# Head-norm averages through 32-wide groups, other slots for the sample states, and another order in the last pair of a two-layer decoder step

## What is computed

```python
# layer A, per head (4 heads of 256): norm of the gated output h
h = sigmoid(o_pre) * hs
mu = mean(h, axis=-1, keepdims=True)              # over the 256 values of a head
var = mean(square(h - mu), axis=-1, keepdims=True)
hn = (h - mu) * rsqrt(var + EPS) * g_hn
y = hn + skip * xc
# layer A, the samples' states: C (8 samples, 4 heads, 256, 256)
C_new = dc * C + ws * outer(v, k)                 # 32 states, each read, updated and written
num = ... + dec * einsum('vk,k->v', C, q)
# end of either layer
out = concat([y_mix, ym]) @ w_out
x = x + rmsnorm(out, g_post)
```

## Time and profile before

| | us |
|---|---|
| three runs | 1763.52, 1765.01 (median), 1767.86 |
| profiled execution | 1766.36 |
| its span in the trace | 1764.2 |
| busy in it: TensorE, VectorE, ScalarE, GpSimd | 1744.2, 869.8, 592.5, 499.0 |

### The profile page before, as it was taken

How to read it: one execution, slowest core, us unless ns; L and a number is a source line. 1 busy time by engine, 2 the same in 40 slices (tenths; PEclk the granted TensorE clock), 3 DMA queues, 4 the chain that set the end, 5 groups by cost and what they waited for, 6 DMA issues and landing times.

```text
span 1764.2 us, 22648 instructions
## 1 busy us (share of the span) xinstructions
PE 1744.2 (99%) x8390; PEld 1361.2 (77%) x8390; DVE 869.8 (49%) x1801; ACT 592.5 (34%) x1437; POOL 499.0 (28%) x539
## 2 busy tenths in 40 slices
PE   9999999999899999999999999999999999999998
PEld 5577766988788888747658888888888888888643
DVE  1444323785566556552333444355435544466775
ACT  2321235564465234311221223432333234533312
POOL 0251100335222002410003543145414553123630
PEclk9999999999999999999999999999999999999999
DMA  7312111247655235541111111223123343745323
GB/s 270 137 61 79 53 64 57 53 135 174 200 159 173 90 93 150 176 167 48 50 48 59 47 48 44 97 90 96 50 73 117 102 141 109 270 159 167 126 104 112
DMA packets 149079, 196.23 MB, mean 111 GB/s; under 512 B 19083, under 2 KB 108171, under 8 KB 148834
## 3 DMA queue, kind: packets, MB, share of 16 engines
q1 hardware_dynamic: 140708, 174.58, 31.2%
q10 hardware_dynamic: 8262, 20.20, 3.4%
HBM read 156.97 MB, written 37.85 MB: 110 GB/s over the span
## 4 chain that ended last, share of the span: by engine, by line
PE 90%; DVE 3%; issue 3%; ACT 1%; DMA 1%; POOL 1%; DVEq 0%; SPq 0%; ACTq 0%; POOLq 0%
PE PS L3511 51%; PE PS L2257 7%; PE PS L2407 5%; PE PS L2047 3%; PE PS L396 3%; PE PS L570 3%; PE PS L2498 2%; PE PS L2083 2%; PE PS L2058 2%; PE PS L291 2%; PE PS L2080 2%; PE PS L920 1%; DVE WK L727 1%; PE PS L913 1%; PE PS L1337 1%
## 5 line engine op out<-in xcount | busy, mean ns | idle before, releaser
L3511 PE MATMUL PS<-HT,RING 128*128 128x258 f32 (+2 forms) x1776 | 444.6, 381 | 0.3 <-ACT WK L3601 0.3
L3511 PEld LDWEIGHTS PS<-HT,RING 128*128 128x128 f32 x1776 | 329.5, 190 | 46.0 <-issue 1.1
L3601 ACT ACTIVATE BIG<-PS 128x256 f32<-128x256 f32 (+2 forms) x140 | 53.8, 385 | 382.3 <-PE PS L3511 382.2
L3511 PE MATMUL PS<-BIG,RING 128*128 128x258 f32 (+1 forms) x656 | 159.6, 382 | 0.0
L3511 PEld LDWEIGHTS PS<-BIG,RING 128*128 128x128 f32 x656 | 123.1, 190 | 17.9 <-issue 0.2
L3511 PE MATMUL PS<-BIG,WK 128*128 128x258 f32 (+1 forms) x448 | 114.2, 386 | 5.2 <-DVE BIG L3703 5.2
L3511 PE MATMUL PS<-HT,CST 128*128 128x256 f32 (+2 forms) x432 | 110.2, 382 | 0.1
L3511 PEld LDWEIGHTS PS<-BIG,WK 128*128 128x128 f32 x448 | 84.3, 193 | 17.9 <-DVE BIG L3703 5.6
L3511 PEld LDWEIGHTS PS<-HT,CST 128*128 128x128 f32 x432 | 79.6, 190 | 11.5 <-DVE BIG L3700 0.9
L570 PE MATMUL PS<-WK,RING 128*128 128x344 f32 x288 | 84.3, 453 | 0.1
L3697 DVE TENSOR_TENSOR BIG<-BIG,PS 128x256 f32<-128x256 f32 (+1 forms) x70 | 29.6, 422 | 104.8 <-PE PS L3511 104.8
(11 more groups left out here) (452 smaller groups left out, 3255.5 us busy)
## 6 DMA issues: line engine op xcount, KB each, us to landing
RING<-in_w_in_a SPq DMA_DIRECT2D x14, 1024.0 KB, 6.2
WK<-in_cache_mem_kv SPq DMA_DIRECT2D x56, 256.0 KB, 5.7
RING<-in_w_kv_b SPq DMA_DIRECT2D x12, 1024.0 KB, 5.3
RING<-in_w_in_b SPq DMA_DIRECT2D x12, 1024.0 KB, 5.2
WK<-in_cache_win SPq DMA_DIRECT2D x40, 256.0 KB, 5.1
RING<-in_w_mkv SPq DMA_DIRECT2D x16, 512.0 KB, 5.1
BIG<-in_x_prompt SPq DMA_DIRECT2D x16, 512.0 KB
BIG<-sample_query SPq DMA_DIRECT2D x28, 256.0 KB, 5.7
```

Of the source, the lines that this page charges most:

```text
L3511: last = nc.tensor.matmul(PS[:, bank, 0:mid - lo], weight_block(u // 2, s, k), h_block(layer_of(u), u % 2, t, k), start=(k == 0 and j not ...
L3601: nc.scalar.activation(part(u, n2 if j == 0 else n1, lo, mid), PS[:, banks(u)[0], 0:mid - lo], ACT.Copy).then_inc(sig("projections_copied" ...
```

## The change

Three edits.

First, an average is made in two steps. `group_sums` multiplies four quarters of the columns (258 each) with 32 columns of the averaging matrix, each quarter into 32 other partitions of bank 7; ScalarE copies them back to SBUF, scaled by 1/32 (`group_sums_act`); in the slot behind, `average` multiplies each 32 rows with ones and writes them to four banks (3 to 6) on all partitions. The root's Ln moves to VAR + 2, to the slot of its Exp.

Second, the states' slots come from a formula. For n = 0 to 23 they were 9, 12, 16, 19, 23, 26, 30, 33, 37, 40, 44, 47, 51, 54, 58, 61, 65, 68, 72, 75, 79, 82, 86, 89. They are 9, 12, 16, 24, 27, 30, 34, 37, 41, 44, 47, 51, 54, 58, 61, 64, 68, 71, 75, 78, 81, 85, 88, 92.

Third, product 2 of the last pair goes from behind `value(5)` to the end, and for the last block ScalarE and VectorE take the second half first.

```diff
@@ -115,6 +115,9 @@
...
+        def quarters(ap):
+            return ap.rearrange("p (b n) -> p b n", b=4)
+
         def vec(row, kt):
...
@@ -185,7 +188,9 @@
...
         for h in range(H):
+            job(f"sums_mean{h}")
             job(f"mean{h}", "dve")
+            job(f"sums_var{h}")
             job(f"var{h}")
...
@@ -1233,9 +1238,13 @@
...
+        def state_slot(i):
+
+            n = i - EARLY_STATES
+            return (9, 12, 16)[n] if n < 3 else 24 + 17 * (n - 3) // 5
+
         def states_at(x):
-            return [i for i in range(EARLY_STATES, H * NS)
-                    if 9 + 7 * ((i - EARLY_STATES) // 2) + 3 * (i % 2) == x]
+            return [i for i in range(EARLY_STATES, H * NS) if state_slot(i) == x]
...
@@ -1324,17 +1333,33 @@
...
-        AVERAGED = PS[:, 3:6, 0:SEG]
-
-        def average(pe, name, h, summed):
+        QUARTER = W // 4
+        AVERAGED = PS[:, 3:7, 0:QUARTER]
+
+        def group_sums(pe, name, h, summed):
...
                 pe.wait_ge(sig("c_copied").sem, H)
-            else:
+            for q in range(4):
+                last = nc.tensor.matmul(PS[32 * q:32 * (q + 1), 7, 0:QUARTER], avg_h[:, 0:32],
+                                        big(HELD[h][0], q * QUARTER, (q + 1) * QUARTER), start=True, stop=True)
+            last.then_inc(job_done.up(), 1)
+
+        def group_sums_act(act, name, h):
+
+            act.wait_ge(job_done.sem, done("sums_" + name))
+            nc.scalar.activation(big(HELD[h][0], 0, QUARTER), PS[:, 7, 0:QUARTER],
+                                 ACT.Copy, scale=1.0 / 32).then_inc(job_read["act"].up(), 1)
+
+        def average(pe, name, h):
+
+            pe.wait_ge(*read_of("sums_" + name))
+            if name != "mean0":
                 pe.wait_ge(*read_of(f"mean{h}" if name[0] == "v" else f"var{h - 1}"))
-            for b in range(3):
-                last = nc.tensor.matmul(AVERAGED[:, b, :], avg_h, big(HELD[h][0], b * SEG, (b + 1) * SEG),
+            for q in range(4):
+                rows = slice(32 * q, 32 * (q + 1))
+                last = nc.tensor.matmul(AVERAGED[:, q, :], ones[rows, :], big(HELD[h][0], 0, QUARTER)[rows, :],
                                         start=True, stop=True)
...
@@ -1345,10 +1370,16 @@
...
                 if x == MEAN[h]:
-                    average(pe, f"mean{h}", h, "values_summed")
+                    group_sums(pe, f"mean{h}", h, "values_summed")
+                    yield
+                if x == MEAN[h] + 1:
+                    average(pe, f"mean{h}", h)
                     yield
                 if x == VAR[h]:
-                    average(pe, f"var{h}", h, "squares_summed")
+                    group_sums(pe, f"var{h}", h, "squares_summed")
+                    yield
+                if x == VAR[h] + 1:
+                    average(pe, f"var{h}", h)
                     yield
...
@@ -1401,7 +1432,7 @@
...
                 act.wait_ge(sig("y_ready").sem, 2 * h - 1)
-            nc.scalar.activation(seg3(ROOT), AVERAGED, ACT.Ln, bias=EPSC).then_inc(job_read["act"].up(), 1)
+            nc.scalar.activation(quarters(ROOT), AVERAGED, ACT.Ln, bias=EPSC).then_inc(job_read["act"].up(), 1)
...
@@ -1437,11 +1468,14 @@
...
                 for h in range(H):
+                    if x == MEAN[h]:
+                        group_sums_act(act, f"mean{h}", h)
                     if x == GATE[h] + 12:
                         squares_act(act, h)
-                    if x == GATE[h] + 17:
+                    if x == VAR[h]:
+                        group_sums_act(act, f"var{h}", h)
+                    if x == VAR[h] + 2:
                         root_log(act, h)
-                    if x == GATE[h] + 18:
                         root_exp(act, h)
...
@@ -1495,7 +1529,7 @@
...
                 dve.wait_ge(job_done.sem, done(f"mean{h}"))
-                ins = nc.vector.tensor_tensor(seg3(big(6 * h + e)), seg3(big(6 * h + e)), AVERAGED, ALU.subtract)
+                ins = nc.vector.tensor_tensor(quarters(big(6 * h + e)), quarters(big(6 * h + e)), AVERAGED, ALU.subtract)
                 if e == 1:
...
@@ -2307,9 +2341,9 @@
...
                       (0, 4), (0, 1), (5, 2), (0, 3), (0, 5), (0, 6),
-                      (2, 1), (2, 4), (7, 2), (2, 3), (2, 5), (2, 6),
+                      (2, 1), (2, 4), (2, 3), (2, 5), (2, 6),
                       (5, 1), (5, 4), (5, 3), (5, 5), (5, 6),
-                      (7, 1), (7, 4), (7, 3), (7, 5), (7, 6)]
+                      (7, 1), (7, 4), (7, 3), (7, 5), (7, 6), (7, 2)]
...
@@ -2618,7 +2652,6 @@
...
             value(5)
-            pair_product(pe, p3, 2)
             pair_product(pe, p1, 3)
...
@@ -2631,7 +2664,7 @@
...
             pair_product(pe, p2, 6)
-            for j in (1, 4, 3, 5, 6):
+            for j in (1, 4, 3, 5, 6, 2):
                 pair_product(pe, p3, j)
...
@@ -2639,6 +2672,10 @@
...
                 .then_inc(sig("block_root").up(), 1)
+
+        def half_order(x, i):
+
+            return (1, 0) if x == "B" and i == NB - 1 else (0, 1)
...
@@ -2649,12 +2686,12 @@
...
                 act.wait_ge(sig("block_squares").sem, squares_of(x, i - 2, 1))
-            for half in range(2):
+            for k, half in enumerate(half_order(x, i)):
                 if x == "B":
...
                 nc.scalar.activation(junk[0:n, half * 512:(half + 1) * 512], src, ACT.Square,
-                                     accum_out=small(x, i, half)).then_inc(sig("block_squares").up(), 1)
+                                     accum_out=small(x, i, k)).then_inc(sig("block_squares").up(), 1)
             act.wait_ge(sig("block_bias").sem, nth(x, i))
...
@@ -2733,11 +2770,11 @@
...
                 dve.wait_ge(sig("block_sum").sem, nth(x, i - 2))
-            for half in range(2):
-                dve.wait_ge(sig("block_squares").sem, squares_of(x, i, half))
+            for k, half in enumerate(half_order(x, i)):
+                dve.wait_ge(sig("block_squares").sem, squares_of(x, i, k))
                 last = nc.vector.tensor_tensor(c.t(i)[0:n, halves[half]], half_of(i, half), c.post[0:n, halves[half]],
                                                ALU.mult)
-                if half == 0:
+                if k == 0:
                     nc.vector.tensor_scalar(small(x, i, 2), small(x, i, 0), 1.0 / D, EPS, ALU.mult, ALU.add)\
...
```

## The result

The changed kernel takes 1775.65 us (median of 6 runs, 1773.81 to 1779.31), the kernel before 1763.42 beside it (1759.82 to 1767.86). The ratio is 1.0070, with a 95% interval of [1.0053, 1.0088]: 12.3 us slower. The profiled execution took 1779.31 us, its span 1777.5.

A forecast was written before the change was run, and what follows sets the result against it. TensorE was busy 1744.2 of 1764.2 us, so only fewer columns or fewer waits change the time. Terms -8.5 + 11.8 + 6.6 + 1.1 + 0.3 = +11.3 on 1765.0 gave 1776.3 us, range 1767 to 1785.

The forecast's parts named there:

- (f): Whole kernel: the forecast with its small terms, clock falling in two or three waits, 1773 to 1780 us; chance 0.52.
- first wait with its clock: TensorE's wait on the C21 sum near 455, fourth state at slot 19: 5.2 plus 3.3 us go, -8.5.
- three new waits: TensorE waits for U2 at slots 38, 66, 94, behind gating of heads 1 to 3: 4.6, 4.8, 2.4 us, +11.8.
- slow clock behind them: Granted clock falls behind two of the waits for U2, 3.3 us each: +6.6; ends 0 and +9.9.
- averages: Eight averages in narrow groups: 0.83 + 1.05 = 1.88 us each against 1.74, +1.1; ends -0.6 and +9.8.
- last pair: Last stage, product (7, 2) at the end: a 1.9 us wait uncovered behind value step 5, net +0.3; ends -1, +1.
- Rival (a): Gating of heads 1 to 3: ScalarE's last sums done before VectorE asks, no new waits; -7.1, 1757.9 us; chance 0.07.
- Rival (b): Clock holds through the waits for U2, or falls once: +4.7 to +8.0, 1769.7 to 1773.0 us; chance 0.15.
- rival (e): The wait near 455 stays, loads late whatever the slot, or slots not as said: 1784.8 us; chance 0.06.
- (c): Narrow groups run at pure column time, 0.86 us per average: -7.0 instead of +1.1, 1768.2 us; chance 0.10.
- (d): The four row groups run one after another: +9.8 instead of +1.1, 1785.0 us; chance 0.10.

The follow-up runs named there:

- repaired slots alone: Kernel before with only the slots of states n = 0 to 7 changed, to 9, 12, 16, 23, 25, 28, 31, 34; ratio 0.9973 to it.
- fourth state early: Changed kernel with state slots 9, 12, 16, 19, 25, 28, 31, 34, then the old ones; ratio 0.9992 to the kernel before.
- slots alone: Kernel before with only the change's new state slots, old averages and old order of the last products; ratio 1.0073 to it.
- kernels with one late head: Changed kernel, slots 9, 12, 16, 23, 25, 28, 31, 34, then old ones, except n = 7 at 37 (1.0019) or n = 23 at 92 (0.9991 to before).
- head 3 alone late: Changed kernel with state slots 9, 12, 16, 23, 25, 28, 31, 34, then old ones, but n = 23 at 92; ratio 0.9991 to before.
- averages computed twice: Changed kernel, slots 9, 12, 16, 23, 25, 28, 31, 34, then old ones, every group sum and average done twice; ratio 1.0013 to before.

## Why the prediction was right, and where it was not

The forecast was 1776.3 us, +11.3, and the median came out at 1775.65, +12.3 by the ratio, in the case that was called likeliest (f). (The kernel before stood at 1763.42 in these runs and not at 1765.0, which is why the time looks closer than the difference.) Step by step:

| term | forecast | measured | by |
|---|---|---|---|
| first wait with its clock | -8.5 | -4.8 (trace: -8.5) | repaired slots alone; -3.7 by the fourth state early |
| three new waits | +11.8 | +12.1 (the same in slots alone) | waits of the trace |
| slow clock behind them | +6.6 | +5.35 | chain, 3 x 42 records |
| averages | +1.1 | -1.0 | chain; alone -0.9 |
| last pair | +0.3 | +0.4 | tail of the trace |
| sum | +11.3 | +12.1 | runs: +12.3 (+9.3 to +15.5) |

**The new waits** are the step that carried the result, and it held in mechanism, place and size. The engine, the two instructions and who queues behind them were as the order had shown. Per head 4.6, 4.8 and 2.4 were forecast, 5.07, 5.13 and 1.91 came. For head 1 VectorE needed longer from the end of the sums (485.30) to the end of U2 (489.6): 4.3 us where 0.79 + 2.50 + 0.42 = 3.7 was reckoned. The steps from L1506 on took 1.01 us for the 0.79, and the two multiplications (L1524) 2.91 for the 2.50 of the earlier trace rows. In the chain of the changed kernel the same stretch is 5.0 us for head 2 and 4.1 for head 3, where 4.6 was reckoned for both, so part of the good sum is that these misses cancel. Rival (a), the one on the other side, fell: ScalarE's 6.34 us of idling ahead of the copy was there, and of no use, since its queue is in order. Rival (b) had the clock fall once or never, and it fell twice; rival (e) had the first wait stay, and it went.

**The first wait** is the mis-sized term. The price was taken from one execution, 5.17 + 3.3. The place and the cause were right, and in that trace the number was too; but over runs it is about 4 us (4.8 and 3.7 by the two comparisons). The step that failed is the one that set the sum "against the profiled execution" and then moved it to the median by 1.35 us: a wait that was 0.4 to 5.2 us in four executions can't be moved to the median by one constant. The earlier trace rows had the sign of it: GpSimd had idled 17.95 us there until a DMA landed, so the wait's length was set by a load's arrival and not only by instructions of fixed duration.

**The clock.** It fell behind two of the three, as taken, but the price of the one row (3.3) was the high one: 3.13, 1.95 and 0.27 came, and 2.4 and 1.95 in the kernels with one late head. My reason (two waits are nearly as long as the one seen, the third is half that) gave the right answer in the changed kernel by luck: with head 3 alone late the clock fell behind 1.90 us.

**The averages** had the wrong sign, and the measured -1.0 lies just outside the ends (-0.6 to +9.8). The edge was about right (0.33 and 0.42 for 0.40). The step that failed is the 0.65 for the column time of the row groups, reasoned from 128-column weight loads: it measured 0.43, with the same weight loads in it, and that makes 1.8 of the 2.1 us. Rivals (c) and (d), -7.0 and +9.8, both fell, by the averages computed twice.

**The last pair** went as worked out: 1.86 us of wait for 1.9, 13.98 us for the four products at the end in one piece, no sum between them and the last squares.

The near agreement of the total is partly luck: the first wait was forecast as 3.7 us too large a gain, the clock as 1.25 and the averages as 2.1 too large a loss, and these 3.7 and 3.35 cancel.

## What to carry to other kernels

When steps are moved by a table of slots, look for the in-order queue in which a moved step now stands behind another, and for who waits for it: 18 later slots cost nothing that the runs show, and three that crossed one instruction cost 17.5 us. A wait that ends on a load's arrival should be priced from several executions, or as a range from nothing to the row's value, while one that is made of instructions can be added up from rows (5.07, 5.13 and 1.9 us in two kernels alike), to some half a us. The narrow form paid here per visit, not per instruction, so gather the work of several visits into one.

## What the runs showed of the hardware

- Four column groups of 32 and four row groups of 32, each of 258 columns, ran at four times the wide form's rate in this kernel, 0.44 and 0.43 us for a set of eight records where six wide ones take 1.74; entering and leaving cost 0.33 and 0.42 us.
- The granted clock behind a wait of TensorE is not set by that wait's length alone: behind 1.90 us it was 0.66 once (the 42 records took 11.09 us) and 1.00 two other times (9.41), behind 2.52 us it held at 1.00 (2.45 us for ten records), and behind 4.41 to 5.7 us it fell each of seven times, for 1.9 to 3.3 us. Waits equal to 0.01 us in two kernels were followed by 3.1 and 2.4, and by 1.95 and 3.2 us of loss.
- A restart at full clock still cost 0.27 us in the chain, 9.41 - 9.14 for 42 records and 2.45 - 2.18 for ten.
- The same state load let GpSimd begin at 448.3, 451.9, 452.0 and 457.1 us into four executions, one each of four kernels, and TensorE's own arrival moved between 450.6 and 456.5; the wait between them went from 5.2 to 0.4 us.
